# Two layer norms turned by diagonal matrices, and a hybrid layer fed from unscaled input

## The chip, the core and the metric

The kernel runs on one core of a Trainium2 chip. Its engines are TensorE (PE, with its weight loads shown as PEld), VectorE (DVE), ScalarE (ACT), GpSimd (POOL) and SyncE (SP), each with an instruction queue of its own; they meet by semaphores. Work memory is the SBUF, results of TensorE land in eight PSUM banks of 128 partitions by 512 float32. The metric is the device time of one execution in microseconds (us), lower is better.

## The reference, cut to what matters

One sequence of 256 tokens of 1024 features passes a retention layer, a latent-attention layer and a hybrid layer. The first two end in a residual add and a layer norm; the third begins with an RMS norm of what the second layer norm gives.

```python
def _layer_norm(x, g, b, eps=1e-5):
    mu = mean(x); var = mean(square(x - mu))
    return ((x - mu) * rsqrt(var + eps)) * g + b

def first_block(x, ...):
    for layer in range(2):
        y = _retention_layer(...) if layer == 0 else _mla_layer(...)
        x = _layer_norm(DEEPNORM_ALPHA * x + y, ln_g[layer], ln_b[layer])

def hybrid_layer(x, norm1_w, w_in, ...):
    h = rms_norm(x, norm1_w)
    u = h @ w_in
    rnn_x, rnn_gate, q, k, v, iq, ik, iw, g = split(u)
    q, k, ik = rms_norm per head of 64 columns   # v, iq, iw as they are
    ...
    x = x + merged @ w_out                        # the layer's input is needed again here
```

## The kernel before

**Numbers.** Every large product is float32 work done as three passes of the faster float32r type: each operand is split into a high and a low part, and `mm3` issues high by high, high by low and low by high. So each weight block ("unit", 128x2048) arrives by a DMA of SP in one of four raw slots, ACT writes its high part (`act_hi`, L841), DVE its low part (`dve_lo`, L1257), and TensorE takes it. 148 units pass in a fixed order; ACT and DVE work three units ahead (`AHEAD`), and a slot is free again when its unit has been used.

**Turned activations.** Products want the activations with features on the partitions (`xT`, high and low part, 8 tiles of 256 tokens). They come from the token-major `res` (2 tiles of 128 tokens) by 128x128 transposes on TensorE (`pe_turn_pair`, L388): four of them fill a bank with a pair of feature tiles; ACT reads the bank as high part (`act_turned`), DVE subtracts for the low part (`dve_turned`). The semaphores are `turned`, `turned_hi` and `turned_lo`.

**The end of a layer.** `pe_output` finishes tokens 0-127 first (two column blocks of 512), then tokens 128-255. `dve_layer_norm` adds each block to `res` as it is done (L1398), takes statistics (L1400, L1404) and the reciprocal root (`dve_root`, with the square root itself on ACT, L865). Tokens 0-127 are then scaled on ACT (L952) and multiplied by g and added to b on POOL (L1832, L1834); tokens 128-255 are done on DVE (L1414, L1427). Only then can TensorE turn. Meanwhile it runs products that nobody reads (`keep_warm`, L380: 20 after the first layer, 36 after the second, each 128x512).

**The hybrid layer's start.** After the second layer norm ACT sums squares (L1059), DVE makes the root, ACT and DVE write the scaled `c_h` (L1065, L1580), TensorE turns it, and ACT and DVE split it with `norm1_w` as a factor per feature (L859, L1278). Then `pe_hybrid` runs blocks b = 0 to 3 of queries, keys, values and index queries (units 80 to 87, two each, `token_major`), the index keys (`c_kw`, 48 small products), and four feature-major units for the recurrence (88 to 91). ACT and DVE each copy half of every block out of PSUM (`c_drain_a`, `c_drain_v`). After unit 88 TensorE turns queries and index queries in banks 4 to 7 and, two pairs later, waits until ACT has read a bank (`small_read`).

**The queues.** Each engine's program is written out by hand and runs strictly in its written order; nothing reorders it.

Of the kernel before, what the change touches and what calls it, by code (L numbers as in the profile page):

```python
# [10 lines left out]
P = 128  # L11
# [26 lines left out]
             ("conv_w_2", 32), ("gate_b_2", 16), ("head_norms", 3))  # L38
# [3 lines left out]
WARM = (20, 36)  # L42
# [10 lines left out]
TURN = {"a": 0, "qlat": 4, "lat": 7, "h": 9, "ya": 13, "res": 17}  # L53
# [16 lines left out]
    "o_prod", "ln_shift", "ln_scaled", "ln_t0", "ln_t1",  # L70
# [4 lines left out]
    "c_sq", "c_total", "c_h0", "c_h1", "c_drain_a", "c_drain_v", "c_kw_hi", "c_kw_lo", "c_sp_in", "c_sp_exp", "c_zeros",  # L75
# [85 lines left out]
def place_retention(k):  # L161
# [228 lines left out]


def pe_program(k):
# [17 lines left out]
    keep_warm(k, WARM[1])  # L410
# [321 lines left out]

def pe_hybrid(k):
    T, s, ps = k.T, k.s, k.ps
    for n in range(4):
        T.wait_ge(s["c_h0"], n // 2 + 1)
        T.wait_ge(s["c_h1"], n // 2 + 1)
        pe_turn_pair(k, "h", n, lambda t, c: k.c_h[:, t, c * P:(c + 1) * P], ps[:, 4 + n, :])
# [8 lines left out]
    T.wait_ge(s["c_kw_lo"], 1)  # L747
    for n in range(KD):
        for t in range(NT):
            x = tuple(z[:, n, t * P:(t + 1) * P] for z in k.xT)  # L750
            m = mm3(k, ps[:, 4 + t, 0:2 * ID + IH], x, tuple(z[:, n, :] for z in k.c_kw), n == 0, n == KD - 1)
    m.then_inc(s["c_ikw_mm"], 1)

    T.wait_ge(s["c_drain_a"], 4)
    T.wait_ge(s["c_drain_v"], 4)
    for n in range(4):
        if n == 1:
            T.wait_ge(s["c_ikw"], 1)
# [11 lines left out]
        feature_major(k, U_RNNX + n, k.xT, KD, S, halves(ps[:, n, :]))  # L770
# [1245 lines left out]
```

## Time and profile before

| what | value |
|---|---|
| median of three runs | 938.85 us (937.69 to 939.58) |
| the profiled execution | 938.36 us |
| its span | 937.0 us |
| TensorE busy | 919.2 us (98%) |
| VectorE busy | 582.0 us (62%) |
| ScalarE busy | 496.4 us (53%) |
| GpSimd busy | 91.2 us (10%) |
| TensorE clock granted, mean | 0.995 of full |

The profile is of one execution; 1.4 us of its time lie outside the span. "PE busy" counts the 56 products that nobody reads as work. In a timeline row the first number is the start, the second the time from the first start to the last end of the merged instructions, and "[3.18 <-DVE res L1427]" says that the engine stood idle for 3.18 us before it and who released it. Matmuls are pipelined, so the pace of a stream is the distance between starts and not the length of one. A plain float32 matmul is recorded as two, so L700 with x2 is one instruction.

### The profile page before, as it was taken

Reading aid. Unit: us, or ns where it says so; the run is one execution under the profiler, and the core shown is the slowest. Engines: PE = TensorE matmul, PEld = TensorE weight load, DVE = VectorE, ACT = ScalarE, POOL = GpSimd, SP = SyncE. Lnnn points to the kernel's source line nnn. Section 1 sums busy time; section 2 is a strip of 40 time slices with the busy share of each in tenths; the row PEclk is TensorE's granted clock in tenths of the full one; section 3 lists DMA queues with packets and bytes.
Section 4 is the critical chain, followed back from the end, with each engine's and each line's share of the span. In section 5 each row is a group of like instructions: output and inputs, shape, how many; then the busy total and the mean of one; then the engine's idle time right before and its main releaser. Section 6 shows DMA issues by size and latency. Waiting matters only on the chain.

```text
span 937.0 us, 14041 instructions
## 1 busy us (share of the span) xinstructions
PE 919.2 (98%) x5964; PEld 840.5 (90%) x5964; DVE 582.0 (62%) x769; ACT 496.4 (53%) x616; POOL 91.2 (10%) x68
## 2 busy tenths in 40 slices
PE   9999999999999999999989999999998999999998
PEld 8798897879899999998868899999998899998886
DVE  5866576467866666665476668776656665555441
ACT  6445445335766666664335566877653455554330
POOL 0010110020001111111020000111200012220000
PEclk9999999999999999999999999999999999999999
DMA  9834455533454443455534525342344635556520
GB/s 355 321 139 175 165 195 208 162 112 128 168 183 141 141 142 143 145 182 217 181 159 180 191 97 191 109 135 91 112 159 135 225 135 184 182 189 211 182 110 23
DMA packets 24830, 154.67 MB, mean 165 GB/s; under 512 B 3136, under 2 KB 3520, under 8 KB 9024
## 3 DMA queue, kind: packets, MB, share of 16 engines
q1 hardware_dynamic: 22880, 148.97, 44.3%
q10 hardware_dynamic: 1728, 4.28, 1.5%
q8 instruction: 47, 0.77, 0.3%
q0 software_dynamic: 160, 0.52, 0.1%
q14 instruction: 15, 0.12, 0.0%
HBM read 152.72 MB, written 1.05 MB: 164 GB/s over the span
## 4 chain that ended last, share of the span: by engine, by line
PE 85%; ACT 6%; DVE 5%; issue 3%; DMA 1%; SPq 0%; DVEq 0%; ACTq 0%
PE ps L332 25%; PE ps L334 25%; PE ps L333 25%; ACT w_hi_ring L841 2%; ACT c_p L1216 2%; PE ps L553 1%; PE ps L554 1%; PE ps L388 1%; PE ps L574 1%; DMA w_raw<-in_a_w_in 1%; DVE w_lo_ring L1257 1%; PE ps L564 1%; PE ps L460 1%; PE ps L680 1%; DVE c_p L1776 1%
## 5 line engine op out<-in xcount | busy, mean ns | idle before, releaser
L1257 DVE TENSOR_TENSOR w_lo_ring<-w_raw,w_hi_ring 128x2048 fp32r<-128x2048 f32 x146 | 342.1, 2353 | 222.6 <-ACT w_hi_ring L841 222.3
L841 ACT ACTIVATE w_hi_ring<-w_raw 128x2048 fp32r<-128x2048 f32 x146 | 277.9, 1910 | 129.7 <-PE ps L334 124.1
L332 PE MATMUL ps<-xT_hi,w_hi_ring 128*128 128x256 f32 x776 | 222.2, 286 | 0.7 <-DVE w_lo_ring L1263 0.7
L334 PE MATMUL ps<-xT_hi,w_lo_ring 128*128 128x256 f32 x776 | 219.5, 283 | 0.0
L333 PE MATMUL ps<-xT_lo,w_hi_ring 128*128 128x256 f32 x776 | 219.4, 283 | 0.0
L332 PEld LDWEIGHTS ps<-xT_hi,w_hi_ring 128*128 128x128 f32 x776 | 148.6, 191 | 2.3 <-issue 1.5
L333 PEld LDWEIGHTS ps<-xT_lo,w_hi_ring 128*128 128x128 f32 x776 | 148.7, 192 | 0.7
L334 PEld LDWEIGHTS ps<-xT_hi,w_lo_ring 128*128 128x128 f32 x776 | 148.6, 191 | 0.0
L332 PE MATMUL ps<-w_hi_ring,xT_hi 128*128 128x512 f32 (+1 forms) x272 | 107.4, 395 | 0.0
L334 PE MATMUL ps<-w_hi_ring,xT_lo 128*128 128x512 f32 (+1 forms) x272 | 104.7, 385 | 0.0
L333 PE MATMUL ps<-w_lo_ring,xT_hi 128*128 128x512 f32 (+1 forms) x272 | 104.6, 385 | 0.0
L333 PEld LDWEIGHTS ps<-w_lo_ring,xT_hi 128*128 128x128 f32 x272 | 51.6, 190 | 9.7 <-issue 1.0
L332 PEld LDWEIGHTS ps<-w_hi_ring,xT_hi 128*128 128x128 f32 x272 | 51.6, 190 | 9.6 <-issue 1.0
L334 PEld LDWEIGHTS ps<-w_hi_ring,xT_lo 128*128 128x128 f32 x272 | 51.4, 189 | 9.7
L332 PE MATMUL ps<-w_hi_ring,c_fT_hi 128*128 128x512 f32 x128 | 49.8, 389 | 0.0
L333 PE MATMUL ps<-w_lo_ring,c_fT_hi 128*128 128x512 f32 x128 | 49.8, 389 | 0.0
L334 PE MATMUL ps<-w_hi_ring,c_fT_lo 128*128 128x512 f32 x128 | 49.8, 389 | 0.0
L332 PE MATMUL ps<-b_qlatT_hi,w_hi_ring 128*128 128x256 f32 x144 | 41.8, 290 | 0.0
L332 PE MATMUL ps<-c_yT_hi,w_hi_ring 128*128 128x256 f32 x128 | 37.1, 290 | 3.5 <-DVE c_yT_lo L1273 2.6
L334 PE MATMUL ps<-b_qlatT_hi,w_lo_ring 128*128 128x256 f32 x144 | 40.4, 280 | 0.0
L333 PE MATMUL ps<-b_qlatT_lo,w_hi_ring 128*128 128x256 f32 x144 | 40.3, 280 | 0.0
L1894 POOL TENSOR_TENSOR c_fT_lo<-c_fr,c_fT_hi 128x512 fp32r<-128x512 f32 x16 | 20.8, 1301 | 167.1 <-ACT c_fT_hi L1245 167.1
(315 smaller groups left out, 1588.6 us busy)
## 6 DMA issues: line engine op xcount, KB each, us to landing
w_raw<-in_a_w_in SPq DMA_DIRECT2D x22, 1024.0 KB, 4.9
w_raw<-in_w_ff_in SPq DMA_DIRECT2D x16, 1024.0 KB, 4.9
w_raw<-in_w_ff_out SPq DMA_DIRECT2D x16, 1024.0 KB, 4.9
w_raw<-in_b_w_uq SPq DMA_DIRECT2D x16, 576.0 KB, 4.3
w_raw<-in_a_w_out SPq DMA_DIRECT2D x8, 1024.0 KB, 4.8
w_raw<-in_b_w_gate SPq DMA_DIRECT2D x8, 1024.0 KB, 5.0
w_raw<-in_kv_w_up SPq DMA_DIRECT2D x8, 1024.0 KB, 4.8
w_raw<-in_b_w_out SPq DMA_DIRECT2D x8, 1024.0 KB, 5.0
```

The source lines that it names most:

```text
L332: k.T.matmul(out, lh, rh, start=start, stop=False, skip_group_check=True)
L333: k.T.matmul(out, lh, rl, start=False, stop=False, skip_group_check=True)
L334: return k.T.matmul(out, ll, rh, start=False, stop=stop, skip_group_check=True)
L388: m = k.T.transpose(bank[:, (2 * n + t) * P:(2 * n + t + 1) * P], src(t, 2 * pair + n), k.ident[:, :])
L460: m = T.matmul(k.ps[:, 0, cols], k.a_qk[:, 2 + n, e * P:(e + 1) * P], k.a_qk[:, n, e * P:2 * P], start=e == 0 and n == 0, stop=n == 1, ski ...
L553: T.matmul(out, k.b_qn[:, par, h, qs], k.b_kn[:, par, h, keys], start=q == 0, stop=False, skip_group_check=True)
L554: m = T.matmul(out, k.b_qr[:, par, qs], k.b_kr[:, h, keys], start=False, stop=True, skip_group_check=True)
L564: m = T.transpose(k.ps[:, 6, n * P:(n + 1) * P], k.b_p[:, h, n * P:(n + 1) * P], k.ident[:, :])
L841: k.A.activation(k.hi[:, u % RING, :], k.raw[u % RING][:, :], ACT.Copy).then_inc(k.s["w_hi"], 1)
L1216: m = A.activation(k.c_p[:, r, cols], k.c_p[:, r, cols], ACT.Exp, bias=k.c_smx[:, q, r:r + 1], scale=head_scale(k, g)[:, q, r:r + 1], accu ...
L1257: k.V.tensor_tensor(k.lo[:, u % RING, :], k.raw[u % RING][:, :], k.hi[:, u % RING, :].bitcast(F32), ALU.subtract).then_inc(k.s["w_lo"], 1)
L1894: G.tensor_tensor(k.c_fT[1][:, 2 * n:2 * n + 2, :], k.c_fr[:, n % 4, :, :], k.c_fT[0][:, 2 * n:2 * n + 2, :].bitcast(F32), ALU.subtract).t ...
```

## The change

`keep_warm` is gone. Both layer norms now write a *centred* copy, (res - mean) times a row of weights, and let TensorE multiply by a diagonal matrix that holds the reciprocal root of each token: a matmul with the centred block as weights and the 128x128 diagonal as the moving operand turns and scales in one step (`pe_turn_scaled`). Its bias per feature is added when ACT and DVE read the bank. Feature tiles 0 to 3 are turned first; tiles 4 to 7 are turned between the first and the second unit of the stage that follows.

In the second layer the row of weights is g times `norm1_w`, loaded and multiplied beforehand (`c_n1`), so the products of blocks b = 0 to 3 come from input that still lacks the RMS root, and the copies out of PSUM multiply by it. The residual `res` itself is completed on DVE later (`dve_residual`; for the first layer in `dve_latents`), ACT sums its squares during b = 0 (`act_squares`), and during b = 3 the input is turned a second time from `res` with the RMS root on the diagonal ("hs"), for everything after the queries. The index keys move ahead of b = 3. POOL has no layer norm any more.

```diff
-WARM = (20, 36)
-TURN = {"a": 0, "qlat": 4, "lat": 7, "h": 9, "ya": 13, "res": 17}
+TURN = {"a": 0, "qlat": 4, "lat": 7, "h": 9, "hs": 13, "ya": 17, "res": 21}
+def pe_turn_scaled(k, pairs, banks, t, src, diag):
+    for pair, bank in zip(pairs, banks):
+        for n in range(2):
+            tile = 2 * pair + n
+            m = k.T.matmul(k.ps[:, bank, (2 * n + t) * P:(2 * n + t + 1) * P], src[:, t, tile * P:(tile + 1) * P], diag[:, t, :],
+                           start=t == 0 and n == 0, stop=True, skip_group_check=True)
+        if t == NT - 1:
+            m.then_inc(k.s["turned"], 1)
+def pe_turn_normed(k, layer, b, src, diag):
+    for t in range(NT):
+        k.T.wait_ge(k.s["ln_diag"], 2 * layer + t + 1)
+        k.T.wait_ge(k.s[f"ln_t{t}"], 2 * layer + b + 1)
+        pe_turn_scaled(k, (2 * b, 2 * b + 1), (4 + 2 * b, 5 + 2 * b), t, src, diag)
...
-    keep_warm(k, WARM[0])
-    for n in range(4):
-        T.wait_ge(s["ln_t0"], n // 2 + 1)
-        T.wait_ge(s["ln_t1"], n // 2 + 1)
-        pe_turn_pair(k, "a", n, lambda t, c: k.res[:, t, c * P:(c + 1) * P], ps[:, 4 + n, :])
+    pe_turn_normed(k, 0, 0, k.res, k.a_diag)
     pe_latents(k)
...
     for n in range(4):
         b, half = n // 2, n % 2
+        if n == 1:
+            pe_turn_normed(k, 0, 1, k.res, k.a_diag)
         token_major(k, U_QLAT + n, ...)
...
+        if b == 3:
+            pe_index_keys(k)
         for half in range(2):
+            if b == 0 and half == 1:
+                pe_turn_normed(k, 1, 1, k.c_n, k.c_diag)
             token_major(k, U_QKVI + 2 * b + half, ...)
+            if b == 3:
+                T.wait_ge(s["ln_diag"], 6)
+                if half == 1:
+                    T.wait_ge(s["c_ikw"], 1)
+                for t in range(NT):
+                    pe_turn_scaled(k, (2 * half, 2 * half + 1), HS_BANKS[half], t, k.res, k.c_diag)
...
     add(0, 0)
     add(0, 1)
-    root(0, lambda: add(1, 0))
+    variance(0)
+    centre(0, 0)
+    scale(0)
+    add(1, 0)
+    if meanwhile:
+        meanwhile()
     add(1, 1)
-    root(1, centre)
+    variance(1)
+    centre(1, 0)
+    scale(1)
+    centre(0, 1)
+    centre(1, 1)
+    own.mark(V.tensor_scalar(k.shift[:, :], std[:, :], -0.5, None, ALU.mult))
...
+    def scale(t):
+        V.wait_ge(s["rs_std"], ROOT[f"ln{layer}"] + t + 1)
+        own.mark(V.reciprocal(y[:, col], std[:, col]))
+        own.wait()
+        own.mark(V.tensor_scalar(std[:, col], y[:, col], y[:, col], var[:, col], ALU.mult, ALU.mult))
+        own.wait()
+        own.mark(V.scalar_tensor_tensor(std[:, col], std[:, col], 3.0, y[:, col], ALU.subtract, ALU.mult))
+        own.wait()
+        V.tensor_scalar(diag[:, t, :], k.ident[:, :], std[:, col], -0.5, ALU.mult, ALU.mult).then_inc(s["ln_diag"], 1)
...
+    act_dma(k, "lnw1_in", k.c_n1[:, :], d["k_norm1"].broadcast_to([P, D]))
     act_dma(k, "columns_in", k.c_columns[:, :], d["columns"])
...
     dve_lo(k, U_BOUT + 5 + AHEAD)
+    k.V.wait_ge(k.s["lnw1_in"], 48)
+    k.v_own.mark(k.V.tensor_tensor(k.c_n1[:, :], k.c_n1[:, :], k.lnw[1][:, 0, :], ALU.mult))
     dve_lo(k, U_BOUT + 6 + AHEAD)
...
+def dve_residual(k, t):
+    blocks = [(k.res[:, t, b * 512:(b + 1) * 512], k.lnw[1][:, :, b * 512:(b + 1) * 512]) for b in range(2)]
+    own.wait()
+    for r, w in blocks:
+        own.mark(V.scalar_tensor_tensor(r, r, k.mv[:, t, 0:1], w[:, 0, :], ALU.subtract, ALU.mult))
+    own.wait()
+    for r, w in blocks:
+        V.scalar_tensor_tensor(r, r, k.shift[:, t:t + 1], w[:, 1, :], ALU.mult, ALU.add).then_inc(k.s["ln_res"], 1)
```

**Place 1: TensorE at the end of the retention layer.** Before (the last products of the output, the unread ones, the turning, the first products of the latent stage):

```order
L332 MATMUL ps<-w_hi_ring,a_oT_hi 128x512
L333 MATMUL ps<-w_lo_ring,a_oT_hi 128x512
L334 MATMUL ps<-w_hi_ring,a_oT_lo 128x512
L380 MATMUL ps<-xT_hi 128x512 x20
L388 MATMUL ps<-ident,res 128x128 x16
L332 MATMUL ps<-w_hi_ring,xT_hi 128x384
```

And now, with the semaphores each waits for; the second piece stands 24 products further on:

```order
L338 MATMUL ps<-w_hi_ring,a_oT_lo 128x512
L395 MATMUL ps<-a_diag,res 128x128 [waits ln_t0,ln_diag]
L395 MATMUL ps<-a_diag,res 128x128 x3
L395 MATMUL ps<-a_diag,res 128x128 [waits ln_t1,ln_diag]
L395 MATMUL ps<-a_diag,res 128x128 x3
L336 MATMUL ps<-w_hi_ring,xT_hi 128x384 [waits turned_lo,w_lo]
```

```order
L338 MATMUL ps<-w_hi_ring,xT_lo 128x384
L395 MATMUL ps<-a_diag,res 128x128 [waits ln_t0,ln_diag]
L395 MATMUL ps<-a_diag,res 128x128 x3
L395 MATMUL ps<-a_diag,res 128x128 [waits ln_t1,ln_diag]
L395 MATMUL ps<-a_diag,res 128x128 x3
L336 MATMUL ps<-w_hi_ring,xT_hi 128x384 [waits turned_lo,w_lo]
```

The unread products are gone, sixteen transposes have become eight matmuls ahead of the first unit and eight between the first and the second, and the product behind each eight waits for the low parts. The second layer has the same pattern.

**Place 2: VectorE at the end of the attention layer.** Before:

```order
L1496 TENSOR_TENSOR b_og<-ps,b_gate 128x512 [waits b_oT_lo,b_valued]
L1257 TENSOR_TENSOR w_lo_ring<-w_raw_53,w_hi_ring 128x2048 [waits w_hi]
L1257 TENSOR_TENSOR w_lo_ring<-w_raw_54,w_hi_ring 128x2048 [waits w_hi]
L1398 SCALAR_TENSOR_TENSOR res<-res,ps 128x512 [waits o_prod]
L1400 BN_STATS st<-res 128x6 [waits v_own]
```

Now, where `c_n_149` holds the loaded row of `norm1_w`:

```order
L1581 TENSOR_TENSOR b_og<-ps,b_gate 128x512 [waits b_oT_lo,b_valued]
L1299 TENSOR_TENSOR w_lo_ring<-w_raw_53,w_hi_ring 128x2048 [waits w_hi]
L1627 TENSOR_TENSOR c_n_149<-c_n_149,lnw_111 128x1024 [waits lnw1_in]
L1299 TENSOR_TENSOR w_lo_ring<-w_raw_54,w_hi_ring 128x2048 [waits w_hi]
L1444 SCALAR_TENSOR_TENSOR res<-res,ps 128x512 [waits o_prod]
L1446 BN_STATS st<-res 128x6 [waits v_own]
```

A multiply of 1024 columns that waits for a DMA (`lnw1_in`) now stands ahead of the last weight split and of the whole layer norm.

**Place 3: ScalarE around the last block of the hybrid layer's queries.** Before:

```order
L841 ACTIVATE w_hi_ring<-w_raw_55 128x2048 [waits w_used,w_landed2]
L1080 ACTIVATE c_iq<-ps 128x512 [waits w_used]
L1089 ACTIVATE c_ikw<-ps 128x136 [waits c_ikw_mm]
L1089 ACTIVATE c_ikw<-ps 128x136
L1095 ACTIVATE c_junk<-c_qk 128x1024 [waits c_ikw,c_drain_v]
```

Now (`norms` is the root that the copy multiplies by, `c_columns` holds `norm1_w`):

```order
L871 ACTIVATE w_hi_ring<-w_raw_55 128x2048 [waits w_used,w_landed2]
L892 ACTIVATE xT_hi<-ps,c_columns 128x256 [waits turned]
L892 ACTIVATE xT_hi<-ps,c_columns 128x256
L892 ACTIVATE xT_hi<-ps,c_columns 128x256 [waits turned]
L892 ACTIVATE xT_hi<-ps,c_columns 128x256
L1126 ACTIVATE c_iq<-ps,norms 128x512 [waits w_used]
L1137 ACTIVATE c_junk<-c_qk 128x1024 [waits c_ikw,c_drain_v]
```

The index keys' copy has moved up, and four reads of the second turning now stand ahead of the copy of `c_iq` and of the squares for the head norms.

## Rows read from the trace of the kernel before

**Rows 1.** The page's first part: busy us, share of the span, instructions.
```profile
PE 919.2 (98%) x5964; PEld 840.5 (90%) x5964; DVE 582.0 (62%) x769; ACT 496.4 (53%) x616; POOL 91.2 (10%) x68
```

**Rows 2.** TensorE's waits: total us, times, longest.
```profile
PE ps L388 <- ACT c_h L1065: 4.1, 1, 4.1
PE ps L388 <- DVE res L1427: 3.2, 1, 3.2
```

**Rows 3.** Timeline of TensorE between the first two layers.
```profile
204.99 4.70 PE L380 MATMUL ps<-xT_hi 128*128 128x512 f32 x20
212.86 2.44 PE L388 MATMUL ps<-ident,res 128*128 128x128 f32 x16 [3.18 <-DVE res L1427]
215.00 0.66 PE L332 MATMUL ps<-w_hi_ring,xT_hi 128*128 128x384 f32 x1
```

**Rows 4.** Windows: length, busy us of each engine, granted clock, DMA share, GB/s.
```profile
215.00:217.60 2.60, 2.60 (x10) 2.60 (x9) 1.66 (x3) 2.37 (x3) 0.00 (x0) 0.51 0.02 6
490.50:494.00 3.50, 3.43 (x17) 3.46 (x18) 1.62 (x5) 2.86 (x7) 0.00 (x0) 0.52 0.00 0
```

**Rows 5.** Timeline of VectorE in the first layer norm.
```profile
205.19 0.69 DVE L1398 SCALAR_TENSOR_TENSOR res<-res,ps 128x512 f32<-128x512 f32 x1 [0.28 <-PE ps L334]
206.88 0.15 DVE L1286 TENSOR_SCALAR norms<-mv 128x1 f32<-128x1 f32 x1
211.97 1.42 DVE L1427 SCALAR_TENSOR_TENSOR res<-res,norms,lnw 128x512 f32<-128x512 f32 x2
```

**Rows 6.** Timelines: a 128x128 scaling, and both splits of turned tiles with factors.
```profile
551.53 0.29 DVE L1614 TENSOR_SCALAR c_ikw<-c_ikw,c_hr 128x128 f32<-128x128 f32 x1
491.65 3.40 ACT L859 ACTIVATE xT_hi<-ps,c_columns 128x256 fp32r<-128x256 f32 x8 [0.61 <-PE ps L388]
492.52 3.44 DVE L1278 SCALAR_TENSOR_TENSOR xT_lo<-ps,c_columns,xT_hi 128x256 fp32r<-128x256 f32 x8 [1.88 <-ACT xT_hi L859]
```

**Rows 7.** Timeline of TensorE: transposes, then float32 matmuls in attention.
```profile
548.66 1.04 PE L673 MATMUL ps<-ident,c_iq 128*128 128x128 f32 x8
...
621.62 0.38 PE L700 MATMUL ps<-c_kz,c_qT 128*128 128x128 f32 x2
621.84 0.60 PE L702 MATMUL ps<-c_kz,c_qT 128*128 128x256 f32 x2
```

**Rows 8.** Timeline of TensorE between attention and hybrid layer.
```profile
478.11 8.32 PE L380 MATMUL ps<-xT_hi 128*128 128x512 f32 x36
...
493.83 0.58 PE L332 MATMUL ps<-w_hi_ring,xT_hi 128*128 128x512 f32 x1
```

**Rows 9.** Timeline of VectorE around the second layer norm.
```profile
464.00 2.29 DVE L1257 TENSOR_TENSOR w_lo_ring<-w_raw,w_hi_ring 128x2048 fp32r<-128x2048 f32 x1 [3.25 <-ACT w_hi_ring L841]
469.44 2.29 DVE L1257 TENSOR_TENSOR w_lo_ring<-w_raw,w_hi_ring 128x2048 fp32r<-128x2048 f32 x1 [3.15 <-ACT w_hi_ring L841]
...
478.31 0.69 DVE L1398 SCALAR_TENSOR_TENSOR res<-res,ps 128x512 f32<-128x512 f32 x1 [0.28 <-PE ps L334]
```

**Rows 10.** An issue of ACT's queue, and DMA issues of 440:500: KB, us to landing.
```profile
463.19 0.46 ACTq L869 DMA_DIRECT2D lnw<-in_ln_b  x1
...
c_rgw<-in_rg_w ACTq DMA_DIRECT2D x1, 1024.0 KB, 11.0
...
lnw<-in_ln_b ACTq DMA_DIRECT2D x1, 512.0 KB, 6.3
```

**Rows 11.** Timeline of VectorE: low part of the index keys' weights.
```profile
522.71 1.28 DVE L1601 TENSOR_TENSOR c_kw_lo<-c_kw_raw,c_kw_hi 128x1088 fp32r<-128x1088 f32 x1
```

**Rows 12.** Timelines of TensorE and ScalarE at the recurrence's first units.
```profile
542.86 0.33 PE L332 MATMUL ps<-xT_hi,w_hi_ring 128*128 128x256 f32 x1
...
556.16 1.04 PE L673 MATMUL ps<-ident,c_qk 128*128 128x128 f32 x8
...
543.61 2.01 ACT L1095 ACTIVATE c_junk<-c_qk 128x1024 f32<-128x1024 f32 x2
...
554.41 1.07 ACT L1175 ACTIVATE c_iqT<-ps 128x512 f32<-128x512 f32 x2
```

More of the change, by code:

```diff
@@ L857, in act_turned @@
     for n in range(2):
-        tile = 2 * pair + n
-        m = k.A.activation(hi[:, tile, :], bank[:, n * S:(n + 1) * S], ACT.Copy, scale=weight[:, tile:tile + 1])
+        tile, z = 2 * pair + n, bank[:, n * S:(n + 1) * S]
+        if shift is not None:
+            m = k.A.activation(hi[:, tile, :], z, ACT.Identity, bias=shift[:, tile:tile + 1])
+        else:
+            m = k.A.activation(hi[:, tile, :], z, ACT.Copy, scale=weight[:, tile:tile + 1])
     m.then_inc(k.s["turned_hi"], 1)
@@ L904, in act_program @@
     act_attention_output(k)
-    act_layer_norm(k, 1)
+    for t in range(NT):
+        act_root(k, ROOT["ln1"] + t, [z[:, t:t + 1] for z in k.tmp])
     act_hybrid(k)
@@ L1050, in act_attention_output, with act_squares @@
     act_hi(k, U_BOUT + 6 + AHEAD)
+def act_squares(k):
+    A, s = k.A, k.s
+    for t in range(NT):
+        for b in range(2):
+            cols = slice(b * 512, (b + 1) * 512)
+            A.wait_ge(s["ln_res"], 2 * t + b + 1)
+            m = A.activation(k.c_junk[:, t, cols], k.res[:, t, cols], ACT.Square, accum_out=k.c_squares[:, b, t:t + 1])
+    m.then_inc(s["c_sq"], 1)
+    act_root(k, ROOT["rms"], k.tmp)
 def act_hybrid(k):
@@ L1072, in act_hybrid @@
+        act_hi(k, U_QKVI + 2 * b + 1 + AHEAD)
+        if b == 0:
+            A.wait_ge(s["c_total"], 1)
+        elif b == 3:
+            for n in range(2):
+                act_turned(k, "hs", 2 + n, ps[:, HS_BANKS[1][n], :], k.xT[0], vec["norm1_w_2"])
         A.wait_ge(s["w_used"], U_QKVI + 2 * b + 2)
-        bank = ps[:, 2 * (b % 2), :]
+        bank, root = ps[:, 2 * (b % 2), :], k.rs[:, 0:1]
         if b < 2:
-            m = A.activation(k.c_qk[:, 0, b * 512:(b + 1) * 512], bank, ACT.Copy)
+            m = A.activation(k.c_qk[:, 0, b * 512:(b + 1) * 512], bank, ACT.Copy, scale=root)
@@ L1264, in dve_piece, with dve_turned @@
         k.s["first_lo"], 1)
-def dve_turned(k, name, pair, bank, xT, weight=None):
+def dve_turned(k, name, pair, bank, xT, weight=None, shift=None):
     k.V.wait_ge(k.s["turned_hi"], TURN[name] + pair + 1)
     hi, lo = xT
-    if weight is None:
+    factor, op = (weight, ALU.mult) if shift is None else (shift, ALU.add)
+    if factor is None:
         tiles = slice(2 * pair, 2 * pair + 2)
@@ L1400, in add, with variance @@
         own.mark(V.bn_stats(k.st[:, t, b, :], r))
-    def root(t, meanwhile):
+    def variance(t):
         own.wait()
@@ L1405, in root @@
         own.wait()
[L1406 to L1414 removed]
+        V.tensor_scalar(var[:, t:t + 1], k.mv[:, t, 1:2], 1.0, 1e-5, ALU.mult, ALU.add).then_inc(s["rs_var"], 1)
@@ L1435, in dve_latents @@
         dve_lo(k, U_QLAT + n + AHEAD)
+        if n < NT:
+            own.wait()
+            for b in range(2):
+                r = k.res[:, n, b * 512:(b + 1) * 512]
+                V.wait_ge(s[f"ln_t{n}"], b + 1)
+                own.mark(V.scalar_tensor_tensor(r, r, k.shift[:, n:n + 1], k.lnw[0][:, 1, b * 512:(b + 1) * 512], ALU.mult, ALU.add))
     V.wait_ge(s["b_squared"], 1)
@@ L1587, in dve_hybrid @@
+        dve_lo(k, U_QKVI + 2 * b + 1 + AHEAD)
+        if b == 3:
+            for n in range(2):
+                dve_turned(k, "hs", 2 + n, ps[:, HS_BANKS[1][n], :], k.xT, vec["norm1_w_2"])
         V.wait_ge(s["w_used"], U_QKVI + 2 * b + 2)
-        bank = ps[:, 2 * (b % 2) + 1, :]
+        bank, root = ps[:, 2 * (b % 2) + 1, :], k.rs[:, 1:2]
         if b < 2:
-            m = V.tensor_copy(k.c_qk[:, 1, b * 512:(b + 1) * 512], bank)
+            m = V.tensor_scalar(k.c_qk[:, 1, b * 512:(b + 1) * 512], bank, root, None, ALU.mult)
@@ L1819, in dve_feed_forward @@
             V.scalar_tensor_tensor(r, ps[:, 4 + 2 * b + t, :], k.rs[:, t:t + 1], r, ALU.mult, ALU.add).then_inc(s["ff_done"], 1)
-def pool_layer_norm(k, layer):
-    G, s, own, lnw = k.G, k.s, k.g_own, k.lnw[layer]
-    G.wait_ge(s[f"lnw{layer}_in"], 32)
-    for b in range(2):
-        cols = slice(b * 512, (b + 1) * 512)
-        r = k.res[:, 0, cols]
-        G.wait_ge(s["ln_scaled"], 2 * layer + b + 1)
-        own.mark(G.tensor_tensor(r, r, lnw[:, 0, cols], ALU.mult))
-        own.wait()
-        G.tensor_tensor(r, r, lnw[:, 1, cols], ALU.add).then_inc(s["ln_t0"], 1)
 def pool_oT(k, pair):
```

192 lines of the change are left out of this document (96 added, 96 removed).

## The prediction, made before the changed kernel had run

> **What bounds the kernel now.** I read the page first. TensorE is busy 98% of the span [rows 1], so almost every microsecond is its stream, and a change pays only where it shortens that stream or a gap in it. But part of this busy time is padding: the timeline shows 20 unread products from 204.99 and 36 from 478.11 [rows 3, 8]. The list of TensorE's waits then names the two longest of the middle of the run, 4.1 and 3.2 us, both ahead of the transposes of the two layer norms [rows 2]. Padding and wait together make the true gaps, from the last wanted product to the first product of the next stage: 204.99 to 215.00, which is 10.0 us, and 478.11 to 493.83, which is 15.7 us [rows 3, 8]. Elsewhere the stream goes on nearly unbroken, so what is gained or lost in these gaps and in blocks b = 0 to 3 goes to the end of the run at full value.
>
> **First gap, new start.** The last add of the layer norm starts at 205.19 and its variance is formed at 206.88 [rows 5]; neither moves. After that stand one centring of 512 columns, 0.71 (half of the pair that takes 1.42 [rows 5]), three column operations of 0.15 at a distance of about 0.19, and the diagonal, 0.29 like the 128x128 scaling [rows 6]. That is 206.88 + 0.07 + 0.71 + 0.57 + 0.29 = 208.5, and TensorE follows at about 208.65. POOL no longer works beside DVE here. Two matmuls (0.44) and the way to ACT (0.25) bring the first pair to 209.35; from ACT's start to DVE's the eight-tile row shows 0.87, and DVE takes 3.44/8 = 0.43 a tile [rows 6], so two tiles and the hand-over end at 211.15. Start of the latent stage: 211.15 instead of 215.00, -3.85.
>
> **What is paid back in the first gap.** Eight matmuls now lie between the first and second unit. Their price: L700 is the same instruction, a plain float32 matmul with 128 moving columns, and the next one starts 0.22 after it [rows 7]; 8 x 0.22 = 1.76. Tiles 4 and 5 are then ready two matmuls before the last, and the second unit waits for ACT (0.25 + 0.87) and DVE (0.86) and the hand-over: 2.05 less the 0.44 of the last two matmuls, a new wait of 1.6. DVE's and ACT's one weight split fits into the first unit, since it is ready to run from about 212. Before, all four pairs were split while the stream already ran. The clock: before, the window from 215.0 to 217.6 stood at 0.51 of full [rows 4], which is the lower of the two levels, 1.2 GHz; at half pace that lost 1.3 of 2.6 us. Without the unread products TensorE rests from about 206 to 208.6 and again to 211.15, with 0.9 us of work between. It has at least as much reason to come back slow: I take 1.4, so +0.1 to +0.2; the bounds are 0 and a whole low stretch like that of 490.5 to 494.0, 3.5 us, which costs 1.75. First layer: -3.85 + 1.76 + 1.6 + 0.2 = -0.3. The residual multiplies in the latent stage (four of 0.71) go into DVE's idle time there; if that cover failed, 2.8.
>
> **Second gap, the new load.** VectorE ends a weight split at 466.3 (464.00 + 2.29) and is idle until 469.44 [rows 9]. Into this hole goes the multiply by `norm1_w`, which waits for a third broadcast of 512 KB behind `ln_g` and `ln_b` on ACT's queue. `ln_b`, issued at 463.19, took 6.3 us to land, 469.5 [rows 10]. The trace shows no third broadcast there. It cannot be counted on earlier than 469.5; the far bound is the last transfer of that queue, issued near 465.1 and landed after 11.0 [rows 10], 476.1. I take 471.5, two microseconds behind `ln_b`, as `ln_b` itself was behind `ln_g`. The multiply is 1024/1088 of the one that takes 1.28 [rows 11], 1.2. Then the split of 2.29, so the first add starts at 474.95; before it could start at about 471.7, where the split of 469.44 ends. The chain was able to absorb little of it: its four adds and statistics (1.32 each pair), two variances, centrings, roots and one diagonal take 6.1 us to the last add, which its products allow at 478.31 [rows 9]. Now it comes at 481.05, 2.75 late. The bounds 469.5 and 476.1 turn this into 0.75 and 7.35.
>
> **Second gap, new start.** As in the first: add at 481.05, diagonal at 484.4, first pair at ACT by 485.65 (TensorE has rested long enough to turn at half pace), first product at 487.45. Before 493.83, so -6.4: the scaled copy, sums of squares, second root and `norm1_w` factors have gone from the path. Paid back between units 80 and 81: 1.76, and a wait of 1.45 to 1.6. The clock: before, it was low during the transposes, 0.52 from 490.5 to 494.0 [rows 4], and cost the stream itself one product, 0.2. Now the stream begins without sixteen transposes ahead of it and meets the low clock itself: 1.4, so +1.2 (bounds -0.2 and +1.55, the whole 3.5 us at half). Sum to here: -6.4 + 1.76 + 1.5 + 1.2 = -1.95.
>
> **The second turning.** Sixteen more matmuls stand in b = 3: 16 x 0.22 = 3.5, nothing beside them. Their splits are covered: pairs 0 and 1 by unit 87, pairs 2 and 3 by the first half of unit 88, 24 products of 0.12 (48 of them take the 5.8 us from 542.86 to 548.66 [rows 7, 12]). VectorE in b = 0 gets eight more operations of 0.71, a root and two diagonals, some 7.5 us; by my walk unit 83 finds its low part ready 5 us early, unit 84 about 1.5 and the drain of b = 0 1.0 before TensorE wants the bank, and the index keys' low part, now wanted before b = 3, 1.3 early. These I cost at nothing; the covers are thin, and failed they cost as much as the walk is wrong.
>
> **What is late next.** ACT now reads four tiles and then copies `c_iq` before it squares for the head norms (place 3). Before, the squares began 0.75 us after unit 88 (543.61 against 542.86) and the first read of turned index queries at 554.41 ended at 555.0, while TensorE wanted it at 556.16 [rows 12]: 1.1 to spare. Now pair 3 is ready about 0.1 after unit 88 starts, two pairs of reads and DVE's copy end 2.85 after it: ACT slips 2.1 against TensorE and uses up the 1.1, so +1.0 ahead of L673 in the third unit.
>
> **Sum.** First layer -0.3; second -1.95 + 3.5 + 1.0 = +2.55; together +2.2 on the profiled execution's 938.36, 940.6. The median of the runs lies 0.5 above that execution, and from it the sum would be 941.05; I say 940.8.
>
> A rule speaks more strongly against the change. Rows show transposes at 1.04 for eight, some 0.11 apart without the tail, and the plain matmul at 0.22, twice that [rows 7]. The Trainium skill, "TensorE: Matmul & The Clock Gate", section "Terms", calls the transpose mode four times faster for float32. By the rows the 32 matmuls on the path cost 7.0; by the rule they would cost twice that. The measured pace is of this same form, so I keep it.
>
> **The rivals.**
> *The gaps are worth more (faster).* The `norm1_w` row lands by 469.5, which takes 2.0 from the start, ACT's order does no harm (1.0), and the clock costs nothing extra (1.4): 940.8 - 4.4 = 936.4. It decides at whether the wait on the new load ends before about 469.9. For it: the rest of that queue's data is small. Against: `ln_b` alone landed at 469.5. Chance 0.18.
> *The clock.* Both restarts, and the rests of 1.6 us inside the first units, leave TensorE low for two stretches of 3.5 us each instead of one: +1.75 per layer beyond my 1.4, 944.3. For it: the first restart before was low although 20 unread products had run until 209.7 [rows 3, 4]. Against: those rests are short beside a unit of 24 products at 8.32/36 = 0.23 each [rows 8]. Chance 0.08.
> *VectorE and ScalarE pile up in b = 0 to 2.* The chain residual, squares, root, diagonals, low part of unit 84, drain of b = 0 is 2 us longer than walked and TensorE stands before b = 2: 942.8. For it: spare times of 1.0 and 1.3. Against: over the run the two engines are busy only 62% and 53% [rows 1]. Chance 0.14.
> *A turning matmul costs four transposes,* 0.44: 32 x 0.22 more, 947.8. Against it stands L700. Chance 0.02.
> *The new form changes nothing,* paid back almost exactly (no slip of ACT, half of the load's delay): 938.4. Chance 0.2. My own case, 939.3 to 942.3, has 0.38.
>
> **How the numbers follow.** About 0.2% (1.9 us) is what a measurement of this kernel can tell from no change. Faster: the first rival and a little of the others, 0.2. Same, 937.0 to 940.7: the last rival and the lower half of my case, 0.39. Slower: the rest, 0.41. The range from 937.2 to 943.6 leaves out most of the first rival and of the clock's, about 0.2 together.
>
> **What will show it.** In the profile after: no L380; the first latent product at 6.2 us after the last product of the output, the first of unit 80 at 9.3; L395 at 0.22 apart, 48 of them; a wait of about 1.5 before the second unit of both stages, ended by DVE's low part; the multiply by `norm1_w` starting at 5.2 after the split before it ends; unit 88 starting 1.3 to 1.4 later than before (542.86), and a wait of 1 us in the third unit from ACT. If unit 80 starts 6.5 after the output, the load did no harm; if L395 runs at 0.11 or 0.44, the turning was mis-sized; if TensorE waits for w_lo_ring or the drains in b = 2, the third rival holds.

## The result, and the profile after

| kernel | median us | runs | ratio to the kernel before, 95% interval |
|---|---|---|---|
| before | 939.22 (937.62 to 939.81) | 6 | |
| changed | 943.03 (941.91 to 944.12) | 6 | 1.0046 [1.0035, 1.0057] |
| changed, measured again (run 9) | 943.37 (941.55 to 943.54) | 5 | 1.0048 [1.0035, 1.0060] |

The change makes the kernel 0.46% slower, 3.8 us by the medians. The forecast was 940.8, slower, with a range to 943.6. The profiled execution took 941.97 us, span 940.7: 3.7 above the span of before. In what follows a *rest* is a stretch in which TensorE has nothing to do, and *low time* is time in which its granted clock is 1.2 instead of 2.4 GHz. t = 0 and t = 1 are tokens 0-127 and 128-255.

TensorE's waits first (total us, times, longest), in place of the two of [rows 2]:

```profile
PE ps L336 <- DVE xT_lo L1321: 5.7, 4, 1.5
PE ps L395 <- DVE c_diag L1468: 4.2, 2, 3.6
PE ps L395 <- DVE a_diag L1468: 2.6, 1, 2.6
PE ps L687 <- ACT c_iqT L1217: 1.0, 1, 1.0
```

The first line holds the waits ahead of the first and of the second unit of each stage, the next two those for the diagonals, the last is the wait foretold in the third unit of the recurrence.

TensorE's timeline (start, us, instruction, idle before and releaser) through both gaps answers to [rows 3, 8]:

```profile
204.61 1.05 PE L395 MATMUL ps<-a_diag,res 128*128 128x128 f32 x8
208.27 1.16 PE L395 MATMUL ps<-a_diag,res 128*128 128x128 f32 x8 [2.61 <-DVE a_diag L1468]
210.97 0.66 PE L336 MATMUL ps<-w_hi_ring,xT_hi 128*128 128x384 f32 x1 [1.55 <-DVE xT_lo L1321]
216.70 1.95 PE L395 MATMUL ps<-a_diag,res 128*128 128x128 f32 x16
220.13 0.41 PE L336 MATMUL ps<-w_hi_ring,xT_hi 128*128 128x384 f32 x1 [1.49 <-DVE xT_lo L1321]
...
478.88 1.16 PE L395 MATMUL ps<-c_diag,c_n 128*128 128x128 f32 x8 [0.65 <-DVE c_diag L1468]
483.60 1.90 PE L395 MATMUL ps<-c_diag,c_n 128*128 128x128 f32 x8 [3.55 <-DVE c_diag L1468]
486.73 0.77 PE L336 MATMUL ps<-w_hi_ring,xT_hi 128*128 128x512 f32 x1 [1.23 <-DVE xT_lo L1321]
494.11 1.95 PE L395 MATMUL ps<-c_diag,c_n 128*128 128x128 f32 x16
497.55 0.47 PE L336 MATMUL ps<-w_hi_ring,xT_hi 128*128 128x512 f32 x1 [1.49 <-DVE xT_lo L1321]
```

The first gap is 204.61 to 210.97, 6.4 us instead of 10.0. The second ends at 486.73 instead of 493.83. Behind each first unit stand 3.44 us (216.70 to 220.13, 494.11 to 497.55): eight turning matmuls and a wait of 1.49.

Windows of after (length, busy us of TensorE, granted clock, DMA share, GB/s). The third place is behind a rest ahead of the attention's output, which the change does not touch; before shows the same low clock there (last line):

```profile
210.50:215.00 4.50, 4.03 (x15) 0.62 0.00 0
483.00:491.00 8.00, 6.18 (x19) 0.57 0.00 0
709.00:712.50 3.50, 3.50 (x19) 0.51 0.63 267
```

```profile
705.00:712.00 7.00, 6.42 (x42) 0.76 0.65 206
```

A window's length times the missing share of the clock, doubled, is the time that it stood at 1.2 instead of 2.4 GHz: 8.00 x 0.43 x 2 = 6.9 us at the second gap, where before had 3.4. Over the whole span, worked out in the same way, the low time is 13.6 us in this execution and 10.2 in that of before.

VectorE around the second norm answers to [rows 9]:

```profile
463.96 2.29 DVE L1299 TENSOR_TENSOR w_lo_ring<-w_raw,w_hi_ring 128x2048 fp32r<-128x2048 f32 x1 [3.25 <-ACT w_hi_ring L871]
470.77 1.23 DVE L1627 TENSOR_TENSOR c_n<-c_n,lnw 128x1024 f32<-128x1024 f32 x1 [4.52 <-DMA c_n<-in_k_norm]
471.92 2.28 DVE L1299 TENSOR_TENSOR w_lo_ring<-w_raw,w_hi_ring 128x2048 fp32r<-128x2048 f32 x1
474.12 0.68 DVE L1444 SCALAR_TENSOR_TENSOR res<-res,ps 128x512 f32<-128x512 f32 x1
480.14 0.68 DVE L1444 SCALAR_TENSOR_TENSOR res<-res,ps 128x512 f32<-128x512 f32 x1
483.25 0.29 DVE L1468 TENSOR_SCALAR c_diag<-ident,norms 128x128 f32<-128x128 f32 x1
```

The new load holds the multiply to 470.77, the last add comes at 480.14 instead of 478.31.

And the head norms' chain on ScalarE with what TensorE does beside it, for [rows 12]:

```profile
542.96 1.95 PE L395 MATMUL ps<-c_diag,res 128*128 128x128 f32 x16
544.66 0.36 PE L336 MATMUL ps<-xT_hi,w_hi_ring 128*128 128x256 f32 x1
559.16 1.14 PE L687 MATMUL ps<-ident,c_qk 128*128 128x128 f32 x8 [1.00 <-ACT c_iqT L1217]
```

```profile
545.93 0.71 ACT L1126 ACTIVATE c_iq<-ps,norms 128x512 f32<-128x512 f32 x1
547.72 2.01 ACT L1137 ACTIVATE c_junk<-c_qk 128x1024 f32<-128x1024 f32 x2 [1.07 <-DVE c_iq L1692]
558.51 1.08 ACT L1217 ACTIVATE c_iqT<-ps 128x512 f32<-128x512 f32 x2
```

Unit 88 starts 1.80 later than before, and the squares 3.06 after it instead of 0.75.

**Where the 3.7 us are**, in these two executions. The changed run was 0.38 ahead when the first gap began. Then come +0.2 in the first layer (ScalarE's first squares of the latents start at 224.59 against 224.77), +0.14 up to 464, +1.84 from there to unit 88, +1.3 at L687 (wait 1.0, the rest around it), and +0.57 in the attention's output. The change's own parts are the 0.2, the 1.84 and the 1.3, together 3.3. The 0.57 isn't the change's. Here are the timelines of the stage's first product and of the next stage's, of after and of before:

```profile
708.68 0.36 PE L336 MATMUL ps<-c_yT_hi,w_hi_ring 128*128 128x256 f32 x1 [2.58 <-DVE c_yT_lo L1316]
733.28 0.39 PE L336 MATMUL ps<-w_hi_ring,xT_hi 128*128 128x512 f32 x1
```

```profile
705.58 0.46 PE L332 MATMUL ps<-c_yT_hi,w_hi_ring 128*128 128x256 f32 x1 [2.58 <-DVE c_yT_lo L1273]
729.61 0.39 PE L332 MATMUL ps<-w_hi_ring,xT_hi 128*128 128x512 f32 x1
```

These 192 products take 24.60 us in the one and 24.03 in the other, with one low stretch in each: at full clock they start 0.120 apart here and 0.117 there. A second profile of the changed kernel (run 9) has 24.03 again.

### The profile page after: what moved, and what is told of

It is laid out like the page before. It is cut to its first block, busy times and chain, and to the rows that moved or that the text cites. A ratio compares the mean times of both kernels' runs of the same rounds, so it can differ in the third digit from the quotient of the medians.

```text
span 940.7 us, 14085 instructions
## 1 busy us (share of the span) xinstructions
PE 916.9 (97%) x5972; PEld 838.8 (89%) x5972; DVE 589.2 (63%) x791; ACT 496.3 (53%) x622; POOL 79.6 (8%) x60
## 4 chain that ended last, share of the span: by engine, by line
PE 82%; ACT 7%; DVE 6%; issue 3%; DMA 1%; ACTq 0%; SPq 0%; DVEq 0%
PE ps L336 24%; PE ps L338 24%; PE ps L337 24%; ACT w_hi_ring L871 2%; ACT c_p L1258 2%; PE ps L567 1%; PE ps L568 1%; DVE w_lo_ring L1299 1%; PE ps L588 1%; PE ps L395 1%; DMA c_n<-in_k_norm 1%; PE ps L578 1%; PE ps L472 1%; PE ps L694 1%; DVE xT_lo L1321 1%
## 5 line engine op out<-in xcount | busy, mean ns | idle before, releaser
L338 PE MATMUL ps<-c_yT_hi,w_lo_ring 128*128 128x256 f32 x128 | 36.7, 286 | 0.0
```

The costliest lines, as they stand in the source:

```text
L338: return k.T.matmul(out, ll, rh, start=False, stop=stop, skip_group_check=True)
```

## The experiments

Every kernel is compared by its ratio to runs of the kernel before on its own chip; the changed kernel's is 1.0046 and, in run 9, 1.0048, which I use below. A difference of two ratios is uncertain by some 0.15%, 1.4 us. So I also read each trace.

**1. Padding back into the rests (e1_padded).**

```diff
+WARM = ((11, 6, 0), (14, 5, 0))
...
+def keep_warm(k, products, src, bank=7):
...
         pe_turn_scaled(k, (2 * b, 2 * b + 1), (4 + 2 * b, 5 + 2 * b), t, src, diag)
+        if b == 0:
+            keep_warm(k, WARM[layer][t], (k.a_oT, k.b_oT)[layer][0])
```

> The changed kernel with unread products (128x512, 0.23 us each) put back into its rests: 11 between the turnings of t = 0 and t = 1 and 6 behind them in the first layer, 14 and 5 in the second. Nothing else differs. Theory (the lost clock is the larger part of what I under-priced): the low stretches at 210.9 and at 484 go, the first gives back 1.6 us, the second 1.8 of its products and 0.9 of the turning of t = 1; the mean granted clock rises from 0.989-0.993 to 0.996 or more, and the time falls from 943.0 by 4 to 5.5 us to 937.5-939. Rival (the low clock comes at the restart whatever TensorE did before, as it did at 214.4 in the kernel before behind 20 unread products): clock and time stay within 1 us of 943.0.

Measured: 937.88 us, 0.9993 [0.9984, 1.0002], 0.55% or 5.2 us under the changed kernel; clock 0.997 to 1.0. Windows of its two gaps, and the third rest:

```profile
204.50:215.00 10.50, 10.25 (x58) 1.00 0.01 2
477.50:491.00 13.50, 12.66 (x64) 1.00 0.09 23
706.00:709.50 3.50, 3.50 (x19) 0.53 0.55 234
```

```profile
205.31 2.75 PE L404 MATMUL ps<-a_oT_hi 128*128 128x512 f32 x11
210.86 0.41 PE L337 MATMUL ps<-w_hi_ring,xT_hi 128*128 128x384 f32 x1
218.53 0.41 PE L337 MATMUL ps<-w_hi_ring,xT_hi 128*128 128x384 f32 x1 [1.49 <-DVE xT_lo L1330]
```

The starts hardly move (from the end of the output's products to the first latent product 6.36 in both, to unit 80 8.54 instead of 8.65), the units do: 7.67 from the first to the second unit instead of 9.16, and 8.99 instead of 10.82 in the second layer. These gave what the theory said of them, 1.5 and 1.8; of the 0.9 that it expected from the turning of t = 1 in the second layer the trace shows 0.3 (2.79 instead of 3.13 from there to unit 80). The low time in the norms' rests is the largest part of the loss. The rival falls.

**2. The row loaded early (e2_early_row).**

```diff
+    act_dma(k, "n1_in", k.c_n1[:, :], d["k_norm1"].broadcast_to([P, D]))   # start of act_attention_output
...
-    k.V.wait_ge(k.s["lnw1_in"], 48)
+    k.V.wait_ge(k.s["n1_in"], 32)                                          # the row and ln_g
```

> The changed kernel with the norm1_w row loaded at the start of the output stage of the second attention (its buffer is free there) and the multiply waiting for it and ln_g alone. Theory (the new load holds up the norm): the multiply starts near 466.5 instead of 470.8, the low split after it at 469.4 as before, the last add at 478.3 instead of 480.1, unit 80 starts 1.8 us earlier and the time falls by 1.8 to 941.2. Rival (the chain of roots and diagonals behind the adds sets the start, or the clock gives it back): the last add moves and the time stays within 0.5 of 943.0.

Measured: 940.48 us, 1.0020 [1.0012, 1.0029], -0.28% or 2.6 us. Its VectorE:

```profile
468.60 1.22 DVE L1628 TENSOR_TENSOR c_n<-c_n,lnw 128x1024 f32<-128x1024 f32 x1 [0.98 <-DMA lnw<-in_ln_g]
470.77 2.29 DVE L1299 TENSOR_TENSOR w_lo_ring<-w_raw,w_hi_ring 128x2048 fp32r<-128x2048 f32 x1 [0.95 <-ACT w_hi_ring L871]
479.65 0.69 DVE L1444 SCALAR_TENSOR_TENSOR res<-res,ps 128x512 f32<-128x512 f32 x1 [0.56 <-PE ps L338]
```

This run is 1.4 us later here by the first layer's clock, so distances count: the split waits for ScalarE again and the last add for TensorE, so the load is off the chain. From the last product of the output to unit 80 it takes 7.0 instead of 8.6: 1.7 gained, as the theory had it within 0.2. The time fell by 0.8 more than the theory's 1.8. Nine of the eleven executions stand at a mean clock of 0.991, most of the changed kernel's at 0.989 (run 9); what brought that about isn't shown.

**3. The first layer alone (e3_layer0_only).** The kernel before with `pe_turn_normed`, `dve_norm`, `act_turned` with its shift and the late residual in layer 0 only, and no padding there.

> The kernel before with the change in the first layer's norm alone (no unread products there; the second layer as before). Theory (the first layer's balance is +0.2 us in the profiled execution, -3.9 of start against 1.76 of matmuls, 1.5 of wait and 1.6 of clock): 939.2 to 939.9 against 939.2. Rival (the first layer also brings a further low stretch of the clock in most executions, the 1.1 us by which most runs of the changed kernel lie over its profiled one): 940.3 or more, with a granted clock of 0.993 or lower. My prediction's own figure was -0.3: 938.9.

Measured: 939.05 us, 1.0007 [0.9998, 1.0016]. Its clock was 0.995, 0.993 and 0.991 in three, four and four executions, at means of 938.36, 939.03 and 939.83. In the profiled one (0.995) the span is 937.4 against 937.0. So the balance of the first layer without more low time is +0.2 to +0.4, and theory and rival both hold in part: four of the eleven executions stand at 0.991, lower than any of the kernel before beside them, and each step down is 0.7 to 0.8 us. The interval of the ratio includes no change. Most of the loss is the second layer's.

**4. Turning within the first unit (e4_turn_within).**

```diff
+        if midway is not None and n == 2:
+            midway()          # token_major of the first unit; the eight turning matmuls
```

> The changed kernel with the eight turning matmuls of the second half of the tiles placed within the first unit (after 12 of its 24 products) instead of between the first and second unit, in both layers. Theory (the two waits of 1.49 us are ACT's and DVE's reading of the turned pairs, which the other 12 products, 2.8 us, would cover): both waits go, 943.0 - 3.0 = 940.0. Rival (ACT and DVE are in the weight splits of the unit after next at that time, and the reading comes as late as before): the waits stay at 1 us or more each and the time falls by less than 1.

Measured: 939.48 us, 1.0007 [0.9998, 1.0016], -0.41% or 3.8 us. No wait stands before a second unit any more:

```profile
PE ps L397 <- DVE c_diag L1468: 4.8, 2, 3.5
PE ps L397 <- DVE a_diag L1468: 2.6, 1, 2.6
PE ps L336 <- DVE xT_lo L1321: 2.4, 2, 1.2
```

2.4 us of that line are left of 5.7, those ahead of the first units. The theory holds; that the clock stood at 0.989 in six executions shows that the chain met as much low time as before the edit. In the profiled execution (0.991) none of it lies in the attention's output and 10.2 us in the second norm.

**5. Index queries copied out first (e5_drain_first).** `m.then_inc(s["c_drain_a"])` and `c_drain_v` with their copies go ahead of `*_turned(k, "hs", 2 + n, ...)`.

> The changed kernel with the copies of the index queries out of PSUM put ahead of the reading of the last two turned pairs on ACT and DVE. Theory (the 1.0 us wait ahead of the transposes in the third RNN unit is ACT's order: four tiles and then the copy before the squares): the copy runs while TensorE still turns, ACT is 0.75 us earlier, the wait shrinks to 0.3 and the time falls by 0.7 to 942.3; unit 88 does not start later. Rival (TensorE's start of unit 88 waits for the turned pairs, which now come 0.7 later): nothing gained, 943.0 or slower by up to 0.6.

Measured: 940.17 us, 1.0017 [1.0008, 1.0026], -0.31% or 2.9 us.

```profile
544.52 0.69 ACT L1123 ACTIVATE c_iq<-ps,norms 128x512 f32<-128x512 f32 x1 [2.53 <-PE ps L338]
545.86 1.57 ACT L892 ACTIVATE xT_hi<-ps,c_columns 128x256 fp32r<-128x256 f32 x4 [0.65 <-PE ps L395]
547.29 2.02 ACT L1137 ACTIVATE c_junk<-c_qk 128x1024 f32<-128x1024 f32 x2
```

```profile
559.37 1.04 PE L687 MATMUL ps<-ident,c_qk 128*128 128x128 f32 x8
```

I had seen ScalarE's own order only. The squares also waited 1.07 for VectorE's copy, which stood behind its four tiles; with both copies first that goes too, the wait at L687 is gone and 1.3 us are gained, where the theory had 0.7. Unit 88 does not start later (58.0 after unit 80, 57.9 in the changed kernel). The rest lies in the clock: this profile has no low time in the attention's output (its 192 products take 22.48 us, 1.55 less than in run 9 at the same mean clock of 0.991) and more in the second norm's rests.

**6. Plain transposes of a copy scaled by POOL (e6_pool_scaled).**

```diff
+        G.tensor_scalar(k.c_h[:, t, :], k.res[:, t, :], k.rs[:, t:t + 1], None, ALU.mult).then_inc(s["c_hscaled"], 1)   # pool_hybrid
...
-                    pe_turn_scaled(k, (2 * half, 2 * half + 1), HS_BANKS[half], t, k.res, k.c_diag)
...
+                    pe_turn_pair(k, "hs", 2 * half + n, lambda t, c: k.c_h[:, t, c * P:(c + 1) * P], ps[:, HS_BANKS[half][n], :])
```

> The changed kernel with the second turning done by 16 plain transposes of a copy that POOL (busy 8%) scales with the root, instead of 16 matmuls by a diagonal. Theory (a turning matmul costs 0.22 and a transpose 0.11, both measured start to start): 16 x 0.11 = 1.8 us less on TensorE, 941.2. Rival (POOL's two passes over 1024 columns slow VectorE beside them or come too late): a new wait ahead of unit 87 or before b = 2, no gain or slower.

Measured: 938.89 us, 1.0006 [0.9997, 1.0016], -0.42% or 3.9 us, again with no low clock in the attention's output in its profile.

```profile
509.49 5.97 POOL L1959 TENSOR_SCALAR c_h<-res,norms 128x1024 f32<-128x1024 f32 x2 [45.93 <-DVEq L1674]
```

```profile
543.07 1.03 PE L386 MATMUL ps<-ident,c_h 128*128 128x128 f32 x8
543.86 0.36 PE L336 MATMUL ps<-xT_hi,w_hi_ring 128*128 128x256 f32 x1
```

From unit 81 (498.55) to unit 88 it takes 45.3 instead of 47.1: 1.8 gained, 16 times the price difference of 0.11. The other 2.1 us of the fall are not the edit's price; the output without low clock, 22.69 us for its 192 products instead of 24.03 in run 9, is the largest part of them that the profile shows. A turning of eight tiles now holds the stream 0.79 us instead of 1.70.

**7. The second turning doubled (e7_turn_doubled).** 16 more matmuls of the same form, unread.

> The changed kernel with sixteen more unread matmuls of the turning's form (float32, 128 moving columns) just before the second turning's. Theory (price of 0.22 each, all on TensorE's path): +3.5 us, 946.5, L395's group of the second turning unchanged. Rival (a part of the second turning was hidden in idle time of TensorE, or plain matmuls in a row run at another pace): less than +2.5.

Measured: 945.55 us, 1.0078 [1.0065, 1.0091]. At one mean clock, 0.993, it is 945.35 against 941.81 for the changed kernel, +3.5, as 16 x 0.22 has it (2.8 by the ratios, which mix the clocks). From unit 81 to unit 88 it takes 50.7 instead of 47.1, 3.6 more. Its rows:

```profile
535.96 1.95 PE L783 MATMUL ps<-c_diag,res 128*128 128x128 f32 x16
537.74 1.95 PE L395 MATMUL ps<-c_diag,res 128*128 128x128 f32 x16
```

**8. The kernel before without its padding (e8_before_unpadded).**

```diff
-    keep_warm(k, WARM[0])
-    keep_warm(k, WARM[1])
```

> The kernel before without its 20 and 36 unread products. Theory (they bought clock that the change gave up): low stretches now also while the two layer norms are turned and in the first units behind them, slower by 1.5 to 4 us, 941 to 943, clock 0.992 or lower. Rival (they bought nothing, since the clock fell at 214.4 and 490.6 in spite of them): within 0.5 of 939.2.

Measured: 939.09 us, 1.0003 [0.9994, 1.0011], with a clock of 0.985 to 0.989. The theory falls: the padding that is worth 5.2 us in the changed kernel is worth nothing measurable here.

```profile
209.00:216.00 7.00, 3.48 (x17) 0.51 0.00 0
482.00:493.50 11.50, 3.31 (x17) 0.51 0.00 0
493.50:496.00 2.50, 2.50 (x8) 0.53 0.00 0
```

Of 21 us at half clock only 9.3 are busy, and most of these are transposes. In this kernel more than half of the low time passes while TensorE waits. In the first gap the slow transposes put the first product 1.1 us later (11.1 instead of 10.0 after the output), and the products behind it, which lost 1.3 us to the half clock before, run nearly all at full clock.

**9. The changed kernel again (e9_changed_again).**

> The changed kernel itself, for the same chip conditions as the variants and for the granted clock of more executions. Theory (its low clock comes in whole stretches of 3.4 us, four in the execution profiled first and six in most others): clocks on a grid of about 0.0018 with the time rising 0.8 us or so for each step, most at 0.989. Rival (the clock differs between executions but not the time): times at 0.993 and 0.989 within 0.3 us of one another. Median 942 to 943.

Measured: 943.37 us. With the first six runs, eleven executions:

| mean clock | executions | mean time us |
|---|---|---|
| 0.993 | 3 | 941.81 |
| 0.991 | 1 | 942.78 |
| 0.989 | 7 | 943.50 |

Of the 33 executions of the kernel before beside runs 1 to 4, 18 have 0.994 or 0.995, at 937.9, and 15 have 0.992 or 0.993, at 939.2. So the execution profiled first is one of the quick ones of the changed kernel, and most are 1.7 us longer at a lower clock. The profile of this run (0.991, span 941.5) has its further 3.4 us of low time in the first gap.

**10 to 12. The edits together.**

> The changed kernel with four edits together: norm1_w row loaded early, the second turning by transposes of POOL's copy, the other eight turning matmuls within the first unit, the index queries copied out first. If they add: -1.5 (row, by the trace of its own run) - 3.0 - 1.25 - 1.8 = -7.5 against the changed kernel, 934.5 to 935.5. Rival (shorter chains meet more of the low clock, as the run with the turning within the unit did with five stretches instead of four): 936.5 or more at a clock of 0.989 or lower.

> The same four edits with unread products in the rests of both norms (11 and 6 in each layer). Theory (padding takes away all the low stretches of the two norms, 3.9 us where it stood alone): 931 to 932, clock 0.998. Rival (part of that loss was in the waits that the four edits took away): 933 to 934.5.

> As the run with four edits and padding, and ten more unread products in the rest of 2.58 us ahead of the output of the attention (near 703), which no edit of the change touches. Theory: the last low stretch, near 706, goes, clock 1.0, and 1.5 us less than without it, 929.5 to 930.5. Rival (the padding delays the first product or the stretch only moves to the next rest): within 0.5 of the run without it.

| run | median us | ratio | clock |
|---|---|---|---|
| e10_four_edits | 932.57 | 0.9942 [0.9930, 0.9955] | 0.993, once 0.991 |
| e11_edits_padded | 929.57 | 0.9905 [0.9890, 0.9920] | 0.998, once 0.997 |
| e12_third_rest_padded | 929.43 | 0.9908 [0.9894, 0.9921] | 0.999, once 0.998 |

By the prices that the traces of the single runs gave, 7.5 together, the four edits add up and more: unit 88 starts at 538.59, 7.5 before that of run 9, and of the 3 us beyond it 1.3 are the wait at L687 and most of the rest is the attention's output, without low clock in this profile. By the whole gains of the single runs (2.6, 3.8, 2.9 and 3.9, together 13.2) they do not add: here it is 10.0 by the ratios. The profiles of runs 4, 5 and 6 each had no low time in the attention's output, and that can be gained only once; what else the single gains hold beyond their prices isn't shown. The padding then gives 3.0 by the medians, 3.5 by the ratios, less than the 5.2 it gave alone. That is the rival's direction; the time itself, 929.57, lies below both forecasts, because run 10 did. Run 12, at 0.999, shows that a higher clock is not a gain by itself:

```profile
695.81 2.56 PE L406 MATMUL ps<-xT_hi 128*128 128x512 f32 x10 [1.89 <-DVE c_g L1757]
698.21 0.28 PE L337 MATMUL ps<-c_yT_hi,w_hi_ring 128*128 128x256 f32 x1
```

The padding had to stand behind a wait of 1.89 (its bank is read until then) and held the first product to 698.21; without it that product came at 696.58 and then met 3.4 us of low clock. The one eats the other: nothing measurable is gained, where the theory had 1.5. Run 11 beats both kernels, by 0.95% the one before.

## Why the prediction was right in sign, and short by 2.2 us

The forecast was 940.8, the median is 943.03. The sign was held to be only a little likelier than no change, 0.41 against 0.39, and the measured time lies 0.6 below the top of the range. The terms of the sum one by one:

1. *First start, -3.85.* Measured 10.01 - 6.36 = -3.65. Right.
2. *Eight matmuls 1.76, second wait 1.5 to 1.6, in both stages.* 3.44 together, wait 1.49. Right, and run 4 shows that the wait was avoidable.
3. *Second start, -6.4, held by the load at 471.5.* The row landed 0.7 earlier, the start gained 7.1. Right in mechanism (run 2).
4. *Second turning 3.5.* 3.4 in the profile, 3.5 by doubling it. The transpose that is four times faster for float32 (the Trainium skill, "TensorE: Matmul & The Clock Gate", section "Terms") is not borne out: 0.11 against 0.22 again, twice as fast, and run 6 gains by that factor.
5. *VectorE and ScalarE in b = 0 to 2 hidden.* No wait of TensorE there; the copies out of b = 1 and b = 2 start both 1.80 earlier than before (514.19 and 525.07 against 515.99 and 526.87), so the third rival did not come.
6. *ScalarE's slip, +1.0.* The wait is 1.00, its price with the restart 1.3. The cause was only half named: VectorE's copy counts too (run 5).
7. *The clock, +0.2 and +1.2.* This is the term that was mis-sized most. I priced one loss of 1.4 for each restart, read off [rows 4], and compared it with the loss of before. In the profiled execution the products lost 1.5 in the first layer (1.3 before) and 1.8 in the second (0.2 before): +1.8 instead of +1.4. (The turning of t = 1 at half pace stood in my start of unit 80 and is not counted here.) Seven of eleven executions are 1.7 us longer, at a mean clock of 0.989; if that is all clock, the term is about 3.5 in them. None of these was profiled, so where their further low time lies is not shown. That padding the norms' rests takes off 5.2 us by the ratios (run 1) shows that most of it lies there.
8. *The rest.* Everything else of the change sums to +1.5 in the profiled execution, forecast +0.8. The start of the first gap, the turnings and the waits cost 0.3 more than said and ScalarE's slip 0.3, and the start of unit 80 gained 0.7 more. Some 0.7 us, 0.2 in the first layer and 0.5 in the second, I did not place. The pace of the attention's output adds the 0.57 in this one execution.

The 0.7 that the row's earlier landing gave hid as much of the clock's miss. That the time stayed inside the range owes something to that luck.

What misled me: the clock's loss has two factors, how long it is low and how much of that time is on products. [Rows 4, 8] show both, since before most of the low time of the second gap lay on transposes and idle time and cost 0.2. The change takes these waits and transposes out, so the same low time falls on products. I saw that for one stretch and gave two stretches in each layer 0.08. They came in the second layer in both profiles of the changed kernel, in the first in one of the two. The price of my clock rival, 944.3, was nearer to the median than my sum. The "gaps are worth more" rival failed on its own condition: the multiply started at 470.8, not 469.9.

The Trainium skill, "TensorE: Matmul & The Clock Gate", section "HAM oscillation — how this bites in real kernels", describes a matrix engine that falls back to the low clock whenever work comes in bursts with waits between, and pays each time. The traces agree in kind: there are three rests in each norm, the longest of 3.6 us, and up to 6.8 us of low time around them in windows like 483.00:491.00. The same page, section "What's actually happening", puts the penalty of the slow start under 1% of a typical span and warns that it varies from run to run. Both hold (5.2 of 943 us, and 1.7 between executions of one kernel), but here this is more than the whole change.

**Open.** What decides from run to run whether the low clock comes one time or twice, whether it comes in the attention's output at all, and why the products of that output start 0.117 or 0.120 apart, is not settled. For each of these one and the same program shows both: the changed kernel in its two profiles for the first and the last, run 1 for the second (0.998 in seven executions at 938.1 and 1.0 in three at 936.4).

## What to carry to other kernels

Shortening a chain that the matrix engine waits for can move its low clock from the wait onto the products, as it did here; price both, and pad the rests again when the chain is changed (worth 0 in one kernel, 5.2 us in the other). Judge padding by where the low time falls and what it delays, not by the mean clock: 0.986 cost nothing in run 8, 0.999 gained nothing in run 12. When work is split around a unit, put the second part inside the unit, and where a chain needs two engines' copies, look at both engines' order.

## What the runs showed of the hardware

- The low stretches of TensorE's clock in the two norms and the attention's output measured 3.4, 6.8, 10.2 and, in run 8, 13.7 us. The executions of one kernel stood on a few values of the mean clock (0.993, 0.991, 0.989 for the changed one), 0.7 to 1.3 us apart in time.
- The same 192 products of the attention's output started 0.117 apart in one execution and 0.120 in another of the same kernel, both at full clock: 0.57 us.
- A float32 matmul of 128 moving columns holds the stream 0.22 us, a transpose of the same block 0.11; four such matmuls (eight records) with their tail took 1.16 at full clock and 1.9 to 2.1 at half clock.
- POOL scaled 128x1024 float32 in 3.0 us (two in 5.97, run 6), and TensorE had no wait between 500 and 545 us in that profile.
- A broadcast row of 512 KB landed 7.1 us after its issue as third on its queue, where the second took 6.2.
